# Up weights of the experts loaded through ScalarE's DMA queue instead of SyncE's, in a one-core trunk with eight streamed experts

## What is computed

```python
def moe_swiglu(hn, router_w, w_gate, w_up, w_down):
    ...
    def expert_block(args):
        xblk, e = args
        return (jax.nn.silu(xblk @ w_gate[e]) * (xblk @ w_up[e])) @ w_down[e]
    yb = lax.map(expert_block, (xb, blk_e)).reshape(n_slots, d)
    out = jnp.zeros((t + 1, d), jnp.float32).at[slot_tok].add(yb.astype(jnp.float32) * slot_w[:, None])
```

## Time and profile before

| | |
|---|---|
| median of 3 runs | 1414.27 us (1411.99 to 1415.44) |
| the profiled execution's own time | 1412.82 us |
| its span in the profile | 1411.0 us, granted clock 0.991 |
| PE busy | 1377.2 us, 98% of the span |
| ACT / DVE / POOL busy | 278.2 / 500.5 / 89.2 us |
| q1 (SyncE's loads) | 423.64 MB, 75.1% of the 16 engines' span |
| q10 (ScalarE's DMAs) | 3.38 MB, 0.7% |

### The profile page before, as it was taken

One profiled execution on the slowest core, in us unless ns is written; L12 is line 12 of the kernel. 1 busy time (PEld: TensorE's weight loads), 2 busy tenths in 40 slices (PEclk: granted clock), 3 DMA queues, 4 the chain that ended last, 5 costly groups with the idle time before them and its releaser, 6 DMA issues.

```text
span 1411.0 us, 31798 instructions
## 1 busy us (share of the span) xinstructions
PE 1377.2 (98%) x14487; PEld 759.2 (54%) x14487; DVE 500.5 (35%) x1030; ACT 278.2 (20%) x522; POOL 89.2 (6%) x75
## 2 busy tenths in 40 slices
PE   6999999999999989999999999999999999999997
PEld 6998967999989653333333333333333333333333
DVE  5767355554545345233042042042041141240222
ACT  5640234434455410000000000000000000000002
POOL 4340010000000000000100100100100100100000
PEclk8999999999999999999999999999999999999999
DMA  7542016555553359999999999999999999999991
GB/s 276 180 143 98 4 60 217 194 178 183 173 209 120 157 222 413 405 426 412 393 425 415 399 422 415 396 421 421 401 418 413 411 407 420 410 408 421 407 421 54
DMA packets 92987, 436.32 MB, mean 309 GB/s; under 512 B 5816, under 2 KB 29552, under 8 KB 84544
## 3 DMA queue, kind: packets, MB, share of 16 engines
q1 hardware_dynamic: 87232, 423.64, 75.1%
q0 software_dynamic: 3616, 7.42, 2.2%
q10 hardware_dynamic: 2016, 3.38, 0.7%
HBM read 427.46 MB, written 6.96 MB: 308 GB/s over the span
## 4 chain that ended last, share of the span: by engine, by line
PE 90%; DVE 4%; ACT 3%; issue 1%; DMA 1%; POOL 1%; POOLq 0%; DVEq 0%; ACTq 0%
PE bank L2172 41%; PE bank L2198 13%; PE bank L2201 6%; PE bank L1645 5%; PE bank L1646 5%; PE bank L1647 5%; PE bank L2065 2%; PE bank L1871 2%; PE bank L1681 1%; DVE ws L1057 1%; PE bank L2222 1%; ACT qkv_hi L680 1%; PE bank L1786 1%; PE bank L1769 1%; PE bank L2051 1%
## 5 line engine op out<-in xcount | busy, mean ns | idle before, releaser
L2172 PE MATMUL bank<-ring,xt 128*32 128x448 f32 x6144 | 580.3, 539 | 0.4 <-DVE xt L1546 0.4
L2172 PEld LDWEIGHTS bank<-ring,xt 128*32 128x32 f32 x6144 | 199.7, 110 | 372.4 <-issue 369.5
L1496 DVE TENSOR_TENSOR ws<-ws,bank 64x448 f32<-64x448 f32 x96 | 82.3, 988 | 526.4 <-ACT ws L952 526.4
L2198 PE MATMUL bank<-ring,hidden_turned 128*32 128x512 f32 x1680 | 218.8, 593 | 0.0
L952 ACT ACTIVATE ws<-bank 64x448 f32<-64x448 f32 x96 | 51.9, 540 | 653.5 <-PE bank L2172 653.5
L2201 PE MATMUL bank<-ring,hidden_turned 128*32 128x256 f32 x1680 | 129.2, 379 | 0.0
L2201 PEld LDWEIGHTS bank<-ring,hidden_turned 128*32 128x32 f32 x1680 | 54.6, 110 | 125.6 <-issue 125.6
L1645 PE MATMUL bank<-x_hi,weights_hi 128*128 128x256 f32 x320 | 90.3, 282 | 1.3 <-issue 1.3
L1646 PE MATMUL bank<-x_lo,weights_hi 128*128 128x256 f32 x320 | 90.3, 282 | 0.0
L1647 PE MATMUL bank<-x_hi,weights_lo 128*128 128x256 f32 x320 | 89.4, 279 | 0.0
L1244 DVE TENSOR_TENSOR weights_lo<-weights,weights_hi 128x1024 fp32r<-128x1024 f32 x62 | 73.1, 1221 | 40.4 <-ACT weights_hi L801 40.4
(11 more groups left out here) (340 smaller groups left out, 1399.1 us busy)
## 6 DMA issues: line engine op xcount, KB each, us to landing
ring<-in_moe_w_gate SPq DMA_DIRECT2D x64, 1792.0 KB, 13.4
ring<-in_moe_w_up SPq DMA_DIRECT2D x64, 1792.0 KB, 15.7
ring<-in_moe_w_down SPq DMA_DIRECT2D x64, 1792.0 KB, 14.7
weights<-in_a_w_in SPq DMA_DIRECT2D x7, 2048.0 KB, 9.0
weights<-in_ffn_w_up SPq DMA_DIRECT2D x11, 1024.0 KB, 5.3
weights<-in_ffn_w_gate SPq DMA_DIRECT2D x11, 1024.0 KB, 5.2
weights<-in_ffn_w_down SPq DMA_DIRECT2D x11, 1024.0 KB, 4.9
weights<-in_a_w_out SPq DMA_DIRECT2D x2, 2048.0 KB, 8.0
```

The lines of the kernel that those rows point to most:

```text
L1496: dve.tensor_tensor(to, by_row[0], by_row[1], ALU.mult).then_inc(m_hid, 1)
L2172: m = pe.matmul(by_run(bank[2 * b + c][LANE * g:LANE * g + LANE, 0:2 * PART]), xe[:, kt, LANE * b:LANE * b + LANE], w_[:, c, g % 2], start ...
L2198: pe.matmul(bank[6][LANE * g:LANE * g + LANE, :], hT[h][g // 2][:, r], moving(D * j + 512 * (g % 2), 512), start=begin, stop=end, skip_gro ...
```

## The change

ScalarE gets a helper `up_load` and issues 60 of the 64 loads of up weights; SyncE keeps the other loads in their old order, and the four up loads of the first half of expert 0 as well. Slots, sources, the semaphores waited for before a load and those raised by its landing are the same. In the loop over item 6 ScalarE reads the two expert numbers too. TensorE, VectorE and GpSimd run the same instructions as before.

```diff
@@ e_loads (SyncE)
                 for pair, (free, n) in enumerate(freed):
                     e_load(2 * pair, r2[2 * pair], e_in(mg, e, 1, pair), free, n)
-                    e_load(2 * pair + 1, r2[2 * pair + 1], e_in(mu, e, 1, pair), free, n)
                 if not first:
-                    for part, w in enumerate((mg, mu, mg, mu)):
-                        e_load(4 + part, r2[4 + part], e_in(w, e, 1, 2 + part // 2), m_d, 8 * i + 1 + part)
+                    for part in (0, 2):
+                        e_load(4 + part, r2[4 + part], e_in(mg, e, 1, 2 + part // 2), m_d, 8 * i + 1 + part)
@@ e_next (SyncE)
                 e_load(4, r2[4], e_in(mg, e1, 0, 0), m_gh, 6 * i + 6)
-                e_load(5, r2[5], e_in(mu, e1, 0, 0), m_gh, 6 * i + 6)
                 e_load(6, r2[6], e_in(mg, e1, 0, 1), m_gu, 12 * i + 12)
-                e_load(7, r2[7], e_in(mu, e1, 0, 1), m_gu, 12 * i + 12)
-                for part, w in enumerate((mg, mu, mg, mu)):
-                    e_load(part, r2[part], e_in(w, e1, 0, 2 + part // 2), m_d, 8 * i + 5 + part)
+                for part in (0, 2):
+                    e_load(part, r2[part], e_in(mg, e1, 0, 2 + part // 2), m_d, 8 * i + 5 + part)
@@ ScalarE
-            def item(i, last=False, first=False):
+            def up_load(k, e, hf, pair, free, count):
+                act.wait_ge(free, count)
+                if not isinstance(count, int):
+                    act.sem_inc(m_turn, 1)
+                act.dma_start(r2[k], ins["moe_w_up"][0][bass.ds(e, 1), pair * 256:pair * 256 + 256,
+                                                        hf * HALF:(hf + 1) * HALF].rearrange(
+                                  "e (k p) n -> p (e k) n", p=P)).then_inc(ring_in[k], 16)
+
+            def item(i, e, e1=None, last=False, first=False):
                 if not first:
+                    up_load(1, e, 1, 0, m_gh, 6 * i + 3)
+                    up_load(3, e, 1, 1, m_gu, 12 * i + 6)
+                    up_load(5, e, 1, 2, m_d, 8 * i + 2)
+                    up_load(7, e, 1, 3, m_d, 8 * i + 4)
                     item_out(i - 1)
+                if not last:
+                    up_load(5, e1, 0, 0, m_gh, 6 * i + 6)
                 e_silu(i * 2 + 1)
                 if last:
                     lanes_turned()
                 else:
+                    up_load(7, e1, 0, 1, m_gu, 12 * i + 12)
+                    up_load(1, e1, 0, 2, m_d, 8 * i + 6)
+                    up_load(3, e1, 0, 3, m_d, 8 * i + 8)
                     e_silu(i * 2 + 2)
 
             gathered()
+            for pair, (free, n) in enumerate(((m_gh, 1), (m_gh, 2), (m_gh, 3))):
+                up_load(2 * pair + 1, 0, 1, pair, free, n)
             e_silu(0)
+            up_load(7, 0, 1, 3, m_gu, 6)
```

More of the change, by code:

```diff
@@ L981, in item @@
                 else:
+                    up_load(7, e1, 0, 1, m_gu, 12 * i + 12)
+                    up_load(1, e1, 0, 2, m_d, 8 * i + 6)
+                    up_load(3, e1, 0, 3, m_d, 8 * i + 8)
                     e_silu(i * 2 + 2)
             gathered()
+            for pair, (free, n) in enumerate(((m_gh, 1), (m_gh, 2), (m_gh, 3))):
+                up_load(2 * pair + 1, 0, 1, pair, free, n)
             e_silu(0)
+            up_load(7, 0, 1, 3, m_gu, 6)
             for i in range(E - 2):
-                item(i, first=i == 0)
+                item(i, i, i + 1, first=i == 0)
             act.wait_ge(s_items, 1)
@@ L990, in _ @@
             with act.Fori(E - 2, n_more) as i:
-                item(i)
-            item(n_more, last=True)
+                e = act.value_load(e_item[0:1, bass.ds(i, 1)], min_val=0, max_val=E - 1)
+                e1 = act.value_load(e_item[0:1, bass.ds(i + 1, 1)], min_val=0, max_val=E - 1)
+                item(i, e, e1)
+            item(n_more, E - 1, last=True)
             last_out(n_more)
```

## The result

| | before | changed |
|---|---|---|
| median of the runs | 1412.45 us (13 runs, 1411.64 to 1415.44) | 1420.7 us (13 runs, 1417.01 to 1427.8) |
| ratio, 95% interval | | 1.0061, 1.0048 to 1.0074 |
| profiled execution | 1412.8 us | 1417.43 us, span 1415.6 us |

A forecast was written before the change was run, and what follows sets the result against it. TensorE was taken to set the pace, DMA close behind. Profiled 1412.8 us plus terms of 0 and 1 us for overtaken loads gave 1413.8, plus 1.5 for the median 1415.3 us; range 1411.5 to 1430, likeliest case 1412 to 1418.5.

The forecast's parts named there:

- What bounds the kernel: Expert part from 527 us on: TensorE sets the pace, DMA nearly as slow; smallest load window 27.1 us.
- A: Rival, slower: mixing two queues costs DMA rate; 1% gives 1421 us, 2% 1429, 7% 1471; chance 0.16.
- B: Rival, slower: late gate loads, with DMA run dry, make TensorE stand 6 to 9 us, 1420 to 1424; chance 0.11.
- The 60 issues taken from SyncE and given to ScalarE: Issue work: SyncE loses 24 us, ScalarE gains 30 us, both on engines that wait anyway; effect 0.
- Up 0 is issued late in seven blocks … Stall: 0: Items 1 to 7, behind `e_silu`: up 0 9.1 us late, lands after 11.6 us, 6.4 us in time; stall 0.
- The rule of packets: DMA engines alternate between queues packet by packet; down loads, with longer runs, would lose less than half: 0 to 1 us.
- Gate and down loads can be overtaken: SyncE's loads: about two up loads overtake, adding 8.6 us; latest landing 29.0 us; cost 1 us, 0 to 8.9.
- Two streams, 0%: Both queues on the DMA engines: mixing costs no rate, 0% taken, 7% kept as the end.
- The engines run dry for a while in the early half: Early late-up-0 blocks: DMA may idle up to 2 us until gate 1; cost 0, bound 7 us of slack.
- GpSimd's gather, 0: Gather gets one share in three instead of one in two; 11 us longer with the scatter, within 12 us; cost 0.
- C: Rival, no overtaking: queues served by age, nothing moves, 1414.3 us; included in the 0.70 for 0 to 4 us.
- D: Rival, faster: only if TensorE's pattern itself ran faster; chance 0.03.

The follow-up runs named there:

- up 0 early: Changed kernel with the second halves' up 0 issued ahead of `e_silu` instead of behind it; 1412.78 us, ratio 1.0.
- loads alone: About half of the experts' matmuls left out of three kernels: before 1391.38 us, changed 1396.14 us, up 0 early 1394.54 us.
- halved down loads: Changed kernel with each down load issued as two DMAs of 7168 bytes per partition; 1412.9 us, ratio 1.0002.
- down loads in rows: Changed kernel with each down load written as two rows of 7168 bytes per partition, packet count unchanged; 1421.11 us, ratio 1.0058.

## Why the prediction was wrong, and where it was right

**What bounds the kernel:** right. TensorE sets the pace, nothing could be gained, and the smallest window, 27.1 us, is the number on which the result turned: a landing of 27.1 us cost 0.20 us of waiting, one of 31.4 us 4.79. That the time lies in the stated range is no merit of the sum, which had 1 us for a loss of 8.25. The range was wide for the sake of A and B, and neither was the cause. Nor did the 1.5 us added for the median hold: the median of 13 runs of before, 1412.45 us, is no higher than the profiled execution.

**The 60 issues taken from SyncE and given to ScalarE:** right, 0. With up 0 early the same 60 issues cost nothing (1.0, 0.9991 to 1.0009).

**"Up 0 is issued late in seven blocks … Stall: 0":** this is the step that failed. The lateness, 9.1 us foreseen and 9.0 measured, was right, and up 0 itself, 11.6 us foreseen and 13.6 measured, is in time. But the sum was made for up 0 and up 1 only. Up 2 and up 3 stand behind them in the same queue, so the lateness is handed down to the load that comes last. And it was made with half the engines for each queue. Halves hold beside gates; beside downs and the scatter an up load gets 0.52 of 1.59 MB, a third. With that, up 3 lands after 25 to 31 us in the late blocks of the two profiles, where it took 16.5 in the block of before. The term should have been the 8 us that the moved line gave back; the text had 8.9 us as the worst for this term and the next together, but for other reasons, DMA engines run dry and a late gate or down load.

**The rule of packets:** it was weighed on one side only. It was applied to down loads, to which it is kind, and not to the up loads that pay for it. The rows had left it open; the block above closes it, with 120 packets against 117.

**"Gate and down loads can be overtaken", 1 us:** the mechanism was right, the price was 0. Their landings rose, gates from 13.4 to 17.7 us by the median, the latest of all SyncE's to 23.1 us, against a bound of 29.0, and PE never waited for one. "Such a lateness is paid about once" left out the clock: the pair behind a wait of 4.79 us took 1.6 us longer. The 1 us taken did not come from here.

**Two streams, 0%:** right for the kernel. Gates beside ups move 425 GB/s, as a clean stretch did, and with up 0 early the time is unchanged. The 375 GB/s of the earlier trace rows were no like row, though: the packets of SyncE's queue there were 2.0 KB, and 543 small ones of ScalarE's ran beside them. The 0.4% seen with loads alone has slack to hide in.

**The engines run dry for a while in the early half:** right as to place, and free. From 650 to 700 us their share falls to 0.97 at 385 GB/s from 1.02 at 402; but the kernel with halved down loads shows 0.96 at 380 there and loses nothing.

**GpSimd's gather, 0:** right for the gather itself. What was not asked is what the scatter takes from the others. From the second scatter to GpSimd's next step it is 17.7 instead of 12.4 us, and without the scatters 5 us of the loss are gone, even with the gather moved beside up 3.

**The rivals.** The size was that of B, single waits that add up to 1420 to 1424, and its sign "rate unchanged" was met; but B looked at gate and down slots, and the waits are at up slots. A (rate) fell with the early up 0. C and D did not occur. **The tests it named:** the first failed, since PE stands 2.4 us at the ring. q10 carried 113.48 MB, gates and downs came later with some over 22 us, and up 0 stands right behind the last activation, as said. Up loads did not land sooner than 15 us: 16.4 by the median, 14.9 only once up 0 was early.

**Still open:** why a given block waits in one execution and not in the next, since the profiled executions share the pattern but not the blocks; why the 16 engines end their parts of one load up to 11.4 us apart; and why making seven more blocks late did not raise the loss at all.

## What to carry to other kernels

When an in-order engine with compute of its own takes over the issuing of loads, put each issue ahead of any wait for compute that ends later, and follow the last load of a burst, not the first, to its deadline. When two queues share the DMA engines, work out each one's share by packets and their lengths: the queue with the longer contiguous runs takes more bytes, and the other one's last load pays. Leave room for the slowest DMA engine too: its end, and not the mean share, is the landing.

## What the runs showed of the hardware that was not expected

- A wait of TensorE of 4.79 us was followed by a granted clock of 0.72 over 5 us and cost another 1.6 us; one of 4.59 us (down loads in rows) by 0.50 over 5 us and another 3.1. One of 2.03 us cost another 1.9, one of 1.13 us 0.2.
- A load of 1.835 MB had all but 0.04 MB moved when TensorE began a wait of 4.79 us for it: three of the 16 engines had not ended their parts, and the last ended 11.4 us behind the first.
- Queues take turns by packet whatever its length, here a single contiguous run: 72, 72 and 70 packets in 4 us carried 1.00, 0.52 and 0.07 MB. GpSimd's small packets cost the other queues more than their bytes: the scatter's 0.07 MB took 10.6% of the engines' time and lowered the rate from 425 to 397 GB/s.
- Two contiguous rows of 7168 bytes written as two in the access pattern still went out as one run; two DMAs made two.
- One load in each of seven blocks, issued 9 us late, made a kernel slower by 8 us and five times as uneven: with up 0 early 11 runs spread over 2.4 us, without it 9 runs over 12.4.
